# One more seven-product pair per step in two projections of a float32 block, and a transposition moved by a step

## The reference

```python
x = x + jnp.einsum('btd,de->bte', merged, w_out[l])            # OUT
h = rms_norm(x, norm_ffn[l])
gate_up = jnp.einsum('btd,df->btf', h, w_ffn_in[l])            # FFN_IN, 2048 x 11264
ff_gate, ff_up = jnp.split(gate_up, 2, axis=-1)
x = x + jnp.einsum('btf,fd->btd', jax.nn.silu(ff_gate) * ff_up, w_ffn_out[l])   # FFN_OUT
...
z = h @ w_in                                                   # V_IN: the third v; UG_IN: u and gate
u, v, gate = jnp.split(z, 3, axis=-1)
v = rmsnorm(jax.nn.gelu(v), v_gain)
```

## Time and profile before

| | |
|---|---|
| median of three timed runs | 2147.68 us (2147.39 to 2149.02) |
| span of the profiled execution | 2146.8 us |
| TensorE busy | 2135.6 us, 99% |
| VectorE busy | 1742.5 us, 81% |
| ScalarE busy | 1261.2 us, 59% |
| GpSimd busy | 138.1 us, 6% |
| HBM traffic | 192 GB/s over the span |
| chain that ended last | 96% PE, 2% DVE, 1% DMA |

### The profile page before, as it was taken

The page is one execution under the profiler, slowest core; times in us unless marked ns, Lnnn a source line. Parts: engine busy times, 40 slices in busy tenths (PEclk is TensorE's granted clock), DMA queues, the critical chain, the costliest instruction groups (busy, mean ns, idle before and its releaser), DMA issues.

```text
span 2146.8 us, 30208 instructions
## 1 busy us (share of the span) xinstructions
PE 2135.6 (99%) x10176; PEld 1788.8 (83%) x10176; DVE 1742.5 (81%) x2125; ACT 1261.2 (59%) x1483; POOL 138.1 (6%) x218
## 2 busy tenths in 40 slices
PE   9999999999999999999999999999999999999998
PEld 9988888888888888888888888888888888888886
DVE  6578788666565698999899887787889999999886
ACT  6465455465544665555555555557667666666565
POOL 2022433101000000000000000000000000000000
PEclk9999999999999999999999999999999999999999
DMA  7666555575555566666666666666666666656664
GB/s 254 182 189 211 157 157 150 174 236 174 183 186 181 186 205 199 198 196 198 203 188 196 200 193 199 192 204 187 206 206 187 188 193 194 193 180 208 203 193 152
DMA packets 211513, 412.35 MB, mean 192 GB/s; under 512 B 13176, under 2 KB 13280, under 8 KB 211296
## 3 DMA queue, kind: packets, MB, share of 16 engines
q1 hardware_dynamic: 208608, 402.70, 60.9%
q0 software_dynamic: 1920, 5.31, 0.8%
q10 hardware_dynamic: 896, 3.15, 0.5%
HBM read 409.01 MB, written 3.16 MB: 192 GB/s over the span
## 4 chain that ended last, share of the span: by engine, by line
PE 96%; DVE 2%; DMA 1%; ACT 0%; issue 0%; DVEq 0%; SPq 0%; ACTq 0%
PE gp L1983 49%; PE gp L1915 33%; PE mx L1983 10%; PE mx L2226 1%; PE mx L2110 1%; DVE w_lo L1194 1%; DMA raw<-a_w_out_in 1%; PE mx L2275 1%; DVE t_lo L1426 0%; DVE ff_lo L1193 0%; PE mx L2113 0%; DMA x_tok<-x_in 0%; PE mx L2107 0%; PE mx L2162 0%; PE mx L2206 0%
## 5 line engine op out<-in xcount | busy, mean ns | idle before, releaser
L615 ACT ACTIVATE w_hi<-raw 128x1024 fp32r<-128x1024 f32 x759 | 797.1, 1056 | 681.6 <-PE gp L1915 246.3
L1194 DVE TENSOR_TENSOR w_lo<-raw,w_hi 128x1024 fp32r<-128x1024 f32 x759 | 921.2, 1230 | 233.8 <-ACT w_hi L615 224.1
L1983 PE MATMUL gp<-w_hi,a_hi 128*128 128x512 f32 x1053 | 413.3, 393 | 0.0
L1983 PE MATMUL gp<-w_lo,a_hi 128*128 128x512 f32 x1053 | 410.1, 389 | 0.0
L1983 PE MATMUL gp<-w_hi,a_lo 128*128 128x512 f32 x1053 | 409.8, 389 | 0.0
L1983 PEld LDWEIGHTS gp<-w_hi,a_hi 128*128 128x128 f32 x1053 | 197.7, 188 | 43.0 <-issue 2.9
L1983 PEld LDWEIGHTS gp<-w_lo,a_hi 128*128 128x128 f32 x1053 | 197.6, 188 | 41.4
L1983 PEld LDWEIGHTS gp<-w_hi,a_lo 128*128 128x128 f32 x1053 | 197.8, 188 | 39.8
L1915 PE MATMUL gp<-w_hi,a_hi 128*128 128x512 f32 x576 | 229.9, 399 | 0.0
L1915 PE MATMUL gp<-w_lo,a_hi 128*128 128x512 f32 x576 | 224.6, 390 | 0.0
L1915 PE MATMUL gp<-w_hi,a_lo 128*128 128x512 f32 x576 | 224.3, 389 | 0.0
(11 more groups left out here) (420 smaller groups left out, 3305.3 us busy)
## 6 DMA issues: line engine op xcount, KB each, us to landing
raw<-a_w_in_in SPq DMA_DIRECT2D x192, 512.0 KB, 4.5
raw<-w_ffn_in_in SPq DMA_DIRECT2D x176, 512.0 KB, 4.5
raw<-w_in_in SPq DMA_DIRECT2D x175, 512.0 KB, 3.9
raw<-w_ffn_out_in SPq DMA_DIRECT2D x88, 512.0 KB, 4.6
raw<-a_w_out_in SPq DMA_DIRECT2D x64, 512.0 KB, 4.9
raw<-w_out_in SPq DMA_DIRECT2D x32, 512.0 KB, 4.0
raw<-w_proj_a_in SPq DMA_DIRECT2D x16, 512.0 KB, 4.6
raw<-w_proj_b_in SPq DMA_DIRECT2D x16, 512.0 KB, 4.7
```

The costliest lines, as they stand in the source:

```text
L615: act.activation(w_hi[:, slot], raw[:, slot], ACT.Copy).then_inc(hi_ready, 1)
L1194: dve.tensor_tensor(w_lo[:, slot], raw[:, slot], w_hi[:, slot], ALU.subtract).then_inc(lo_ready, 1)
L1983: ins = pe.matmul(out_, stat[sp_], mov[mp], start=start and p == 0, stop=stop and p == 2, skip_group_check=True)
```

## The change

FFN_IN and V_IN take pair 0 too by seven products in every step but the first (`MIXED_WIDE`). Its weight sums are made in the step before (`coming`: at j = 12 and 13, when unit 16, the next step's first, is four away). Since pair 0 writes `mx` at once, PE waits at a step's start for the parts of the step before, and `turn_ff` and `ff_copy` move from j = 1 of the next step to its last j, 15. The operand sums of pair 0 (`s0_hi`, `s0_lo`) are made once ahead of each projection, from the first four rows. V_IN's last step is written apart from its loop, because it prepares no next one. Of the diff, cut:

```diff
+MIXED_WIDE = (0, 2, 4, 6)
...
+        WIDE = (FFN_IN, V_IN,)
...
-            return MIXED
+            return MIXED_WIDE if k in WIDE else MIXED
...
+        def coming(k, i, j):
+
+            u = (j + RING) // 2
+            if u in mixed(k, i):
+                return mixed(k, i).index(u)
+            if u == S[k].units and k in WIDE and not (isinstance(i, int) and i == S[k].steps - 1):
+                return len(mixed(k, i))
+            return None
...
             def ffn_mid(i, j):
-                if j == 1:
+                if j == S[FFN_IN].pair - 1:
                     ff_copy(i - 1)
...
-                if n:
-                    act.wait_ge(op_ready, op0[FFN_IN if turn == TURN_H2 else V_IN] + 4 * n)
+                if n or turn in SUMS0:
+                    if n:
+                        act.wait_ge(op_ready, op0[FFN_IN if turn == TURN_H2 else V_IN] + 4 * n)
                     for m in range(UK):
...
             def double_ahead(k, i, j):
 
-                u, half = (j + RING) // 2, j % 2
-                if u in mixed(k, i) and half == 0:
-                    weight_sums(k, i, mixed(k, i).index(u), j)
+                n = coming(k, i, j)
+                if n is not None and j % 2 == 0:
+                    weight_sums(k, i, n, j)
                 split(j % RING, after(k, i, RING + j + 1), tiles_ahead(k, i, j))
...
                 elif k == FFN_IN:
-                    pe.wait_ge(tile_hi, i + TURN_FF)
+                    pe.wait_ge(parts_added, dbl(k, i))
...
                 pe.wait_ge(lo_ready, after(k, i, 2 * u + 1))
                 three(mx[:, 0], a11, wt(s0, 0), first, last)
-                three(gp[:, 0, 0], a12, wt(s0, 1), False, False).then_inc(unit_used, 1)
+                if u == 0:
+                    pe.wait_ge(bank_free[0], freed(k, i))
+                three(gp[:, 0, 0], a12, wt(s0, 1), u == 0, False).then_inc(unit_used, 1)
...
-                three(gp[:, 1, 0], s4_, wt(s1, 1), False, False).then_inc(unit_used, 1)
+                if u == 0:
+                    pe.wait_ge(bank_free[1], freed(k, i))
+                three(gp[:, 1, 0], s4_, wt(s1, 1), u == 0, False).then_inc(unit_used, 1)
                 pe.wait_ge(t_lo_ready, pairs(k, i, n + 1))
+                if k == FFN_IN and u == 0:
+                    pe.wait_ge(tile_hi, i + (TURN_FF - 1))
...
             def ffn_turn(i, j):
-                if j == 1:
-                    turn_ff(i - 1)
+                if j == S[FFN_IN].pair - 1:
+                    turn_ff(i - 1, i + 1)
```

More of the change, by code:

```diff
@@ L202, in build @@
         small = new("small", [64])
+        s0_hi = new("s0_hi", [4, P], F32R)
+        s0_lo = new("s0_lo", [4, P], F32R)
         assert top[0] <= nc.sbuf_usable_end, top[0]
@@ L737, in double_ahead @@
             def double_ahead(k, i, j):
-                u, half = (j + RING) // 2, j % 2
-                if u in mixed(k, i) and half == 1:
-                    n = mixed(k, i).index(u)
+                n = coming(k, i, j)
+                if n is not None and j % 2 == 1:
                     act.wait_ge(t_summed, pairs(k, i, n + 1))
@@ L766, in double_step @@
                     double_ahead(k, i, j)
-                    if j >= S[k].pair - 2 and half_done is not None:
+                    if j >= S[k].pair - 2 and half_done is not None and not (k == FFN_IN and j == S[k].pair - 1):
                         half = j - (S[k].pair - 2)
@@ L992, in mid @@
                         stat_hi(n, turn, gain)
-                    if j % units == 5 and n >= 1:
+                    if j % units == 5 and (n >= 1 or n == 0 and turn in SUMS0):
                         mixed_hi(n, turn)
@@ L1049, in rows_hi @@
                     squares(n)
-                if j == 3 and n:
+                if j == 3 and (n or TURN_H3 in SUMS0):
                     mixed_hi(n, TURN_H3)
@@ L1096, in _ @@
             double_step(V_IN, 0, v_out, v_first)
-            with act.Fori(1, S[V_IN].steps) as i:
+            with act.Fori(1, S[V_IN].steps - 1) as i:
                 own.enter(i - 1, 6)
                 double_step(V_IN, i, v_out, no_mid)
-                own.leave(S[V_IN].steps - 1)
+                own.leave(S[V_IN].steps - 2)
+            double_step(V_IN, S[V_IN].steps - 1, v_out, no_mid)
             act.sem_inc(sums, 1)
@@ L1418, in double_ahead @@
             def double_ahead(k, i, j):
-                u, half = (j + RING) // 2, j % 2
-                if u in mixed(k, i) and half == 0:
-                    weight_sums(k, i, mixed(k, i).index(u), j)
+                n = coming(k, i, j)
+                if n is not None and j % 2 == 0:
+                    weight_sums(k, i, n, j)
                 split(j % RING, after(k, i, RING + j + 1), tiles_ahead(k, i, j))
-                if u in mixed(k, i) and half == 1:
-                    dve.wait_ge(t_hi_ready, pairs(k, i, mixed(k, i).index(u) + 1))
+                if n is not None and j % 2 == 1:
+                    dve.wait_ge(t_hi_ready, pairs(k, i, n + 1))
                     dve.tensor_tensor(t_of(k)[2][:], t_of(k)[0][:], t_of(k)[1][:].bitcast(F32), ALU.subtract).then_inc(t_lo_ready, 1)
                     if k in (FFN_OUT, Y_FIRST):
-                        dve.wait_ge(sf_hi_ready, sums_made(k, i, mixed(k, i).index(u)))
+                        dve.wait_ge(sf_hi_ready, sums_made(k, i, n))
                         dve.tensor_tensor(sf_lo[:], sf_sum[:], sf_hi[:].bitcast(F32), ALU.subtract).then_inc(sf_ready, 1)
@@ L1501, in double_loop @@
                 with dve.Fori(begin, end) as i:
-                    own.enter(i - begin, 2 * len(MIXED) + 3)
+                    own.enter(i - begin, 2 * len(mixed(k, i)) + 3)
                     double_step(k, i, head, mid)
@@ L1701, in mid @@
                         stat_lo(n, turn, gain)
-                    if j % units == 6 and n >= 1:
+                    if j % units == 6 and (n >= 1 or n == 0 and turn in SUMS0):
                         mixed_lo(n, turn)
@@ L1782, in _ @@
             double_step(V_IN, 0, nothing, v_first)
-            double_loop(V_IN, 1, S[V_IN].steps, nothing, no_mid)
+            double_loop(V_IN, 1, S[V_IN].steps - 1, nothing, no_mid)
+            double_step(V_IN, S[V_IN].steps - 1, nothing, no_mid)
             def ug_first(i, j):
@@ L1993, in operand, with starts @@
                 return [x_[:, UK * u + kk, m * P:(m + 1) * P] for x_ in (a_hi, a_lo)]
+            def starts(k, i, u, half, m):
+                return u == 0 or u == 1 and 0 in mixed(k, i) and (half, m) == (1, 1)
             def plain_pair(k, i, u, mid):
@@ L2005, in plain_pair @@
                             ins = three(gp[:, half, m], operand(k, i, u, kk, m), [w_[:, slot, kk] for w_ in (w_hi, w_lo)],
-                                        u == 0 and kk == 0, u == end and kk == UK - 1)
+                                        kk == 0 and starts(k, i, u, half, m), u == end and kk == UK - 1)
                         if u == end and m == 0:
@@ L2048, in mixed_pair @@
                 else:
-                    s1_, s2_, s3_, s4_ = [[x_[:, MIXED.index(u), q] for x_ in ((sx_hi, sx_lo) if k == AV else (s_hi, s_lo))]
-                                      for q in range(4)]
+                    s1_, s2_, s3_, s4_ = [[x_[:, q] for x_ in ((sx_hi[:, n], sx_lo[:, n]) if k == AV else s_of(u // 2))]
+                                          for q in range(4)]
                 wt = lambda slot, kk: [w_[:, slot, kk] for w_ in (w_hi, w_lo)]
@@ L2253, in turn_x, with turn_ff @@
                 turn(lambda t, m: xs_tok[:, t, m * P:(m + 1) * P])
-            def turn_ff(i):
-                pe.wait_ge(parts_added, dbl(FFN_IN, i + 1))
+            def turn_ff(i, parts):
+                pe.wait_ge(parts_added, dbl(FFN_IN, parts))
                 pe.wait_ge(parts_read, dbl(FFN_IN, i + 1))
@@ L2310, in fo_first @@
                 if j == 3:
-                    turn_ff(S[FFN_IN].steps - 1)
+                    turn_ff(S[FFN_IN].steps - 1, S[FFN_IN].steps)
             def fo_second(i, j):
```

21 lines of the change are left out of this document (14 added, 7 removed).

## The result

| | before | after |
|---|---|---|
| median | 2147.71 us (2147.39 to 2149.02) | 2198.02 us (2196.48 to 2198.65) |
| ratio | | 1.0233, 95% interval 1.0218 to 1.0247 |
| span of the profiled execution | 2146.8 us | 2195.8 us |

A forecast was written before the change was run, and what follows sets the result against it. VectorE, a second bound 1.15 us behind TensorE, was to take over, with FFN_IN's step at 46.3 us. 2146.8 + 37.8 (FFN_IN) + 7.9 (V_IN) = 2192.5 us, taken as 2192, 2.1% slower; range 2170 to 2206.

The forecast's parts named there:

- The margin of 3.7 us: FFN_IN: PE reaches pair 6's end at S + 30.9, VectorE the parts at 34.6, so PE's lateness would not return.
- FFN_IN, forecast +37.8: FFN_IN in all: 34.4 us for nine cycles, 4.8 at step 0's end, less 1.4 given back in step 10.
- The end of step 0: FFN_IN: the pair prepared there adds 4.32 + 0.65 - 0.21 = 4.8 us, as the wait for PE was only 0.21.
- V_IN, forecast +7.9: V_IN in all: the pair's work and load waits, less lost waits for `w_hi` and PE and 0.9 given back.
- the forecast 3.0, 3.2 and 2.6: V_IN: us added at the end of step 0, in step 1 and in step 2, after waits lost.
- PE's release 2.4 us before the next sums: FFN_IN's step end: the second block ends at 865.95, the next sums start at 868.32, so PE is free 2.4 us earlier.
- PE comes back late: Rival: `w_hi` behind `unit_used` makes VectorE wait at j = 0 to 3, about 1 us in 13 places: 2206 us, 10%.
- the rival of the clock: Rival: clock falls at step ends, 36 matmuls run at 1.2 GHz, 4.5 us lost 13 times: 2250 us, 5%.
- Sooner: Rival: loads land sooner, the three DMA waits vanish, FFN_IN's step is 44.3 us: 2171 us, 15%.
- The lead of 1.15 us: FFN_IN: VectorE's wait for PE before the parts, read as its distance behind TensorE as bound and subtracted per step.
- The forecast of 1.00: Granted clock stays whole through idle of some 3 us at 13 step ends, from a pause at the program's end.
- Faster: Rival: VectorE absorbs the pair and PE saves 13 x 0.68 = 8.8 us: 2138 us, 3%.

The follow-up runs named there:

- short sums: Changed kernel with pair 0's four weight sums and its `t_lo` computed for only 32 of 512 columns: 2151.95 us, ratio 1.0016.
- sooner block: Changed kernel with the second block's addition at j = 14 instead of 15, one `w_lo` fewer before PE's release: 2194.09 us, ratio 1.0214.
- the last try: Changed kernel with four small unused products in PE's pause at the step's end: 2195.96 us, ratio 1.0227.
- seven additions: Kernel before, with seven unread VectorE additions of 128x512 behind block 0 of FFN_IN's first ten steps: 2218.20 us, ratio 1.0327.
- short `t_lo`: Changed kernel with only pair 0's `t_lo` computed for 32 of 512 columns: 2178.01 us, ratio 1.0132.
- three additions: Kernel before, with three unread VectorE additions of 128x512 behind block 0 of FFN_IN's first ten steps: 2174.58 us, ratio 1.0127.
- FFN_IN alone: Changed kernel with pair 0 by seven products in FFN_IN only, V_IN as before: 2188.08 us, ratio 1.0182.

## Why the prediction was right, and where it missed

**The bound.** That VectorE takes over and the step becomes its work plus what it waits for holds: busy 42.5 us (42.9 forecast) in 45.6 to 46.2 (46.3), and no wait for PE at the parts. The short sums and `t_lo` show that its time is paid about one for one over both stages; the sooner block shows that PE's release does not set the step in FFN_IN. Where the clock fell, PE's lateness did come back through `w_hi`, in place of the load waits. The margin of 3.7 us had been worked out at the parts, near the step's end; the same room was assumed, not worked out, for `w_hi` at its start.

**FFN_IN, forecast +37.8.** Measured +36 in the trace of the changed kernel and +40.0 by itself. The end of step 0 was +5.1 (4.8) and a step +3.35 (3.82); of the difference of 0.47, 0.4 is VectorE's busy time. The nine steps are thus 4.2 us under the forecast, but the last one gave back 0.1 us and not 1.4, and another 1.2 us arose in FFN_OUT, forecast as nothing: the sum is close in part because errors cancelled.

**V_IN, forecast +7.9: the term that was mis-sized.** Measured 12.7 in the trace: +2.7, +5.9 and +4.3 for the forecast 3.0, 3.2 and 2.6, and 0.2 given back at the end for 0.9. These 4.8 us are most of the 6 by which the forecast missed. First, I took PE's release 2.4 us before the next sums from FFN_IN; there the product's two instructions stand between. In V_IN there is none: block 1 ends at 1575.10 + 1.28 = 1576.38 and the sums start at 1577.43, 1.05 us later. PE and with it ACT's `w_hi` are late by the rest, and the waits for `w_hi` that I had struck out stayed. With PE let go sooner the steps were 44.86 and 44.83 us, +3.5 and +3.2, close to the forecast. Second, the clock, forecast as whole, fell for some 13 and then six or seven matmuls; with falls of six and none, in the last try, the two steps were together 1.9 us shorter. No run has the late release with a whole clock throughout, so how the rest divides stays open. That is the rival "PE comes back late" together with the rival of the clock, true of V_IN (+5 us), hardly of FFN_IN, where the waits mostly took the place of load waits.

**The loads.** "Sooner" was wrong: no wait before the sums went away for good. Where PE was late they turned into waits for `w_hi`; with PE sooner they were 0.5 to 1.0 us.

**The lead of 1.15 us.** Taking it off the sum gave nearly the right step, but the text called it the distance to the bound, and that holds only for work ahead of the parts. For `t_lo`, which lies between the parts and block 1, there was none. Had VectorE had room for everything, the step would still have been longer than before. In the step that PE starts at 877.79, with the clock whole:

```profile
911.01 0.39 PE L2010 MATMUL gp<-t_lo,a_hi 128*128 128x512 f32 x1
```

```profile
913.91 0.68 DVE L1460 TENSOR_TENSOR c_part<-mx,c_part 128x512 f32<-128x512 f32 x1
...
922.02 1.28 DVE L1475 TENSOR_TENSOR c_part<-gp,c_part 128x512 f32<-128x512 f32 x2
```

PE needs 33.22 us to the last product of pair 6, the parts could follow 0.49 us behind its start, and from there to block 1's end are 9.39 us: 43.1 us, an estimate from these rows, and not 41.8. The three matmuls saved take nothing off this ring. They stand ahead of the point where PE waits for block 1 (9 matmuls for 12), and the 147 from there to the end of pair 6 are the same. What does leave the ring is the transposition, some 0.8 us, which now stands ahead of that point too. An addition placed ahead of the parts, which should be covered, was not tried.

**The clock.** The forecast of 1.00 was wrong, and the earlier trace rows misled: a pause of nearly 3 us at the program's end left the clock whole, of six of 3.04 us in FFN_IN four did not. The same rows have 0.62 in the two us that follow, so the fall was not far off. The Trainium skill (TensorE: Matmul & The Clock Gate, "HAM oscillation — how this bites in real kernels") had said that bursts can start cold. Of FFN_IN's ten, four did. The rival's price was wrong too: in FFN_IN some eight matmuls run at the low level, not 36: 835.45 - 832.13 = 3.3 us for 1.8, so 1.5 us. Where VectorE is the bound the margin swallows most of it (45.97 us behind a fall, 45.73 in the other steps); where PE is, as with three and seven additions, it is paid in full.

**Faster.** The three matmuls saved per pair showed up nowhere: even with the pair nearly free on VectorE the ratio was 1.0016. There VectorE's waits for loads hold the step.

## What to carry to other kernels

A helper engine's idle time before a wait covers only work put ahead of that wait; for work behind it, follow the ring to the point where the main engine is let go, and measure the slack there. When a price is carried from one stage to another, look at which instructions stand between the release and the next step in each. A main engine at 99% can hide that its helper has no room: price the trade by the helper's total, busy plus latency waits, per step. And look at what each pause does to the main engine's clock: pauses of 3 us cost it nothing, 1.5 us or some 2.6 us here (13 matmuls at 0.43 us for 0.227), and what of that reaches the time depends on which engine bounds the stage.

## What the runs showed of the hardware

A GpSimd subtraction of 128x1536 in float32 takes 3.93 us (1.76 on VectorE), and a VectorE addition with both operands in SBUF beside it takes 3.80 us for 0.69: GpSimd ends at 878.86 and the addition at 879.41. The addition just ahead of it, begun 0.05 us before GpSimd, kept its 0.69. The Trainium skill (SBUF — State Buffer, "SBUF: two separate sides") calls the port that the two share an exclusive lock, held for the whole instruction; the trace agrees.

The granted clock after a pause of PE at a step's end fell behind 2 of 11 pauses of 1.5 us (short `t_lo`), 7 of 13 of 1.9 us (sooner block), 2 of 10 of 2.0 to 2.1 us (three additions), 1 of 8 of 2.38 us (the changed kernel and FFN_IN alone), 6 of 9 of 3.0 us (the changed kernel) and 10 of 10 of 4.9 to 5.0 us (seven additions), and was back after some 5 to 14 matmuls. So the length of the last pause alone does not decide it in these runs, and none of these lengths was free of falls.
